# Two-block transformer kernel: last merge and gated outputs kept in PSUM, two steps moved on VectorE and TensorE

## The reference, cut to what matters

```
x   = rmsnorm(x, g_final)                      # end of the first block
h   = rmsnorm(x, g_mix)
xc, gb, gc, q, k, v, g_sw, gate_a, gate_r = split(h @ w_in)
y_a = (gb * conv3(gc * xc)) @ w_a_out          # 8 "mixing" steps
ret = retention(q, k, v)                       # 4 heads of 512 value columns
ret = (ret - mean) * rsqrt(var + eps) * g_ret
y_r = (ret * silu(g_sw)) @ w_r_out
merged = sigmoid(gate_a) * y_a + sigmoid(gate_r) * y_r
x   = x + merged @ w_o
x   = x + (silu(rmsnorm(x) @ w_ff_gate) * (rmsnorm(x) @ w_ff_up)) @ w_ff_down
out = rmsnorm(x, g_final_2)
```

## Time and profile before

| | |
|---|---|
| timed runs | 1609.0, 1609.24, 1611.55 us; median 1609.24 us |
| profiled execution, its own time | 1607.12 us |
| its span, first to last instruction | 1605.1 us |
| busy: PE, DVE, ACT, POOL | 97%, 51%, 19%, 62% of the span |
| mean granted TensorE clock | 0.989 of full speed |

### The profile page before, as it was taken

One profiled execution on the slowest core, in us unless ns is written; L12 is line 12 of the kernel. 1 busy time (PEld: TensorE's weight loads), 2 busy tenths in 40 slices (PEclk: granted clock), 3 DMA queues, 4 the chain that ended last, 5 costly groups with the idle time before them and its releaser, 6 DMA issues.

```text
span 1605.1 us, 19515 instructions
## 1 busy us (share of the span) xinstructions
PE 1560.0 (97%) x7096; PEld 1295.3 (81%) x7096; DVE 820.9 (51%) x833; ACT 303.5 (19%) x471; POOL 988.8 (62%) x784
## 2 busy tenths in 40 slices
PE   6899999999999999999999999999999999999996
PEld 5798888887887888788888888888778888888885
DVE  6775555555407566323246675576577443443014
ACT  3423111110102000212021232221222111111011
POOL 0542666667666666666647466575467666667664
PEclk9799999999999999999999999999999999999998
DMA  9791333333232333333223222232223333332321
GB/s 366 264 359 40 101 91 102 94 92 99 89 99 79 105 91 97 91 112 92 81 83 98 77 84 87 77 93 90 65 74 98 92 97 99 91 103 93 96 100 53
DMA packets 227558, 172.38 MB, mean 107 GB/s; under 512 B 5184, under 2 KB 203968, under 8 KB 226496
## 3 DMA queue, kind: packets, MB, share of 16 engines
q1 hardware_dynamic: 227520, 171.85, 34.3%
HBM read 169.73 MB, written 2.10 MB: 107 GB/s over the span
## 4 chain that ended last, share of the span: by engine, by line
PE 89%; DVE 7%; DMA 2%; issue 1%; ACT 1%; SPq 0%; POOL 0%; DVEq 0%; ACTq 0%; POOLq 0%
PE ps L529 29%; PE ps L533 29%; PE ps L532 29%; DMA mod_early<-in_w_mod 2%; DVE wide_lo L1145 1%; PE ps L573 1%; DVE res L1436 1%; DVE ps L1189 0%; DVE tmp L1268 0%; DVE tmp L1554 0%; DVE act_lo L1368 0%; DVE tmp L1364 0%; DVE act_lo L1262 0%; DVE tmp L1175 0%; DVE tmp L1256 0%
## 5 line engine op out<-in xcount | busy, mean ns | idle before, releaser
L507 POOL TENSOR_TENSOR w_lo<-raw,w_hi 128x1024 fp32r<-128x1024 f32 x248 | 623.3, 2513 | 20.7
L529 PE MATMUL ps<-act_hi,w_hi 128*128 128x512 f32 (+1 forms) x1296 | 505.9, 390 | 6.0 <-DVE act_lo L1368 2.6
L533 PE MATMUL ps<-act_lo,w_hi 128*128 128x512 f32 (+1 forms) x1296 | 501.3, 387 | 0.0
L532 PE MATMUL ps<-act_hi,w_lo 128*128 128x512 f32 (+1 forms) x1296 | 501.3, 387 | 0.0
L504 POOL TENSOR_TENSOR w_hi<-raw,zero 128x1 fp32r<-128x1 f32 x248 | 57.9, 234 | 517.4 <-PE ps L529 517.4
L529 PEld LDWEIGHTS ps<-act_hi,w_hi 128*128 128x128 f32 x1296 | 243.8, 188 | 60.3 <-issue 6.8
L532 PEld LDWEIGHTS ps<-act_hi,w_lo 128*128 128x128 f32 x1296 | 244.0, 188 | 50.4 <-issue 1.4
L533 PEld LDWEIGHTS ps<-act_lo,w_hi 128*128 128x128 f32 x1296 | 243.8, 188 | 49.4
L505 POOL TENSOR_SCALAR w_hi<-raw 128x1023 fp32r<-128x1023 f32 x248 | 267.3, 1078 | 0.0
L529 PE MATMUL ps<-wide_hi,w_hi 128*128 128x512 f32 (+2 forms) x624 | 241.8, 388 | 6.6 <-DVE wide_lo L1145 4.2
L532 PE MATMUL ps<-wide_hi,w_lo 128*128 128x512 f32 (+2 forms) x624 | 240.6, 386 | 0.0
(11 more groups left out here) (193 smaller groups left out, 1462.9 us busy)
## 6 DMA issues: line engine op xcount, KB each, us to landing
raw<-in_w_in SPq DMA_DIRECT2D x88, 512.0 KB, 4.0
raw<-in_w_ffn_up SPq DMA_DIRECT2D x44, 512.0 KB, 3.8
gates<-in_w_mod SPq DMA_DIRECT2D x20, 1024.0 KB, 10.4
raw<-in_w_ffn_down SPq DMA_DIRECT2D x22, 512.0 KB, 3.7
raw<-in_w_ff_gate SPq DMA_DIRECT2D x22, 512.0 KB, 3.9
raw<-in_w_ff_up SPq DMA_DIRECT2D x22, 512.0 KB, 3.9
raw<-in_w_ff_down SPq DMA_DIRECT2D x22, 512.0 KB, 3.7
raw<-in_w_r_out SPq DMA_DIRECT2D x16, 512.0 KB, 3.5
```

The costliest lines, as they stand in the source:

```text
L507: nc.gpsimd.tensor_tensor(w_lo[:, two, :], raw[:, slot, :], f32(w_hi[:, two, :]), SUB).then_inc(split_done, 1)
L529: ins = mm(o, w, a, start=start, stop=False)
L532: mm(o, wl, a, start=False, stop=False)
L533: return mm(o, w, al, start=False, stop=stop)
```

## The change

There are five edits.

1. `norm(1, [2, 3])` stands behind the third mixing tile and no longer behind the second.
2. TensorE's wait for `mix_free` ahead of the gates stands ahead of the third gate tile (the first bank that mixing used, 4) and no longer ahead of the first.
3. DVE's first four `gate_scale` stand ahead of the reciprocal and the eight operations that scale `res`.
4. In every head `gated` and `scaled` write, and ACT's high part and `ret_lo` read, the bank 4 + e of PSUM in place of `tmp`. So the next head's values must not be written there before `ret_ready`: that wait stands ahead of the value products, and the wait for `ret_made` ahead of the fourth projection tile is gone. In the last `ret_out` the first tile waits for the third g_sw scaling only and the second tile for the fourth.
5. In the last merge both operations of DVE write the PSUM bank that the tile came in, and the high and low parts are made from there. So a bank is free only at `merge_ready`, and tiles m = 4 to 7 of the last `ret_out` wait for `merge_ready` m - 3 in place of `mid_free`.

```diff
@@ conv_tiles
-                    if first and u == 0 and s == 1:
+                    if first and u == 0 and s == 2:
                         norm(1, [2, 3])
@@ gates, TensorE
-            pe.wait_ge(mix_free, KT - 1)
             for g in range(4):
+                if g == 2:
+                    pe.wait_ge(mix_free, KT - 1)
@@ head_projections
-                    elif u == 2 * QT - 1:
-                        pe.wait_ge(ret_made, h * VT)
                     tile(ps[:, u, :], base + u, u % 2, act_hi, act_lo).then_inc(qk_done, 1)
                 if isinstance(h, int):
                     pe.wait_ge(key_scale_made, 1)
+                else:
+                    pe.wait_ge(ret_ready, h * VT)
@@ ret_out
                 if last:
-                    pe.wait_ge(gsw_scaled, HEADS * VT)
+                    pe.wait_ge(gsw_scaled, HEADS * VT - 1)
                     pe.wait_ge(o_std, HEADS)
-                    pe.wait_ge(split_done, base + 1)
                     for m, k in [(m, k) for ks in (range(VT - 1), [VT - 1]) for m in range(2) for k in ks]:
+                        if k == 0 and m % 2 == 0:
+                            pe.wait_ge(split_done, base + m // 2 + 1)
+                        if (m, k) == (1, 0):
+                            pe.wait_ge(gsw_scaled, HEADS * VT)
                         pe.wait_ge(ret_ready, h * VT + k + 1)
@@
-                    if m >= 4:
+                    if m >= 4 and last:
+                        pe.wait_ge(merge_ready, m - 3)
+                    elif m >= 4:
                         pe.wait_ge(mid_free, (h + 1) * KT + m - 3)
@@ ScalarE
-                    hi_of(wide_hi[:, S_RET + e, :], tmp[:, e, :], ret_hi_made)
+                    hi_of(wide_hi[:, S_RET + e, :], ps[:, 4 + e, :], ret_hi_made)
...
-                hi_of(wide_hi[:, S_MERGE + m, :], gates[:, m, :], merge_hi_made)
+                hi_of(wide_hi[:, S_MERGE + m, :], ps[:, m % 4, :], merge_hi_made)
@@ VectorE (gate_scale for g in 0 to 3 moved ahead of the scaling of res)
-                    stt(out=tmp[:, e, :], in0=ps[:, 4 + e, :], scalar=col("g_ret_2", h * VT + e), in1=tmp[:, e, :],
+                    stt(out=ps[:, 4 + e, :], in0=ps[:, 4 + e, :], scalar=col("g_ret_2", h * VT + e), in1=tmp[:, e, :],
...
-                    tt(tmp[:, e, :], tmp[:, e, :], tmp[:, 6, :], MUL).then_inc(ret_made, 1)
+                    tt(ps[:, 4 + e, :], ps[:, 4 + e, :], tmp[:, 6, :], MUL).then_inc(ret_made, 1)
...
-                    tt(tmp[:, m % 2, :], ps[:, m % 4, :], gates[:, KT + m, :], MUL).then_inc(mid_free, 1)
+                    scaled_, merged = (ps[:, m % 4, :], ps[:, m % 4, :]) if last else (tmp[:, m % 2, :], gates[:, m, :])
+                    tt(scaled_, ps[:, m % 4, :], gates[:, KT + m, :], MUL).then_inc(mid_free, 1)
                     dve.wait_ge(mid_free, (h + 1) * KT + m + 1)
-                    tt(gates[:, m, :], gates[:, m, :], tmp[:, m % 2, :], ADD).then_inc(mid_added, 1)
+                    tt(merged, gates[:, m, :], scaled_, ADD).then_inc(mid_added, 1)
```

More of the change, by code:

```diff
@@ L831, in ret_out @@
                 if last:
-                    pe.wait_ge(gsw_scaled, HEADS * VT)
+                    pe.wait_ge(gsw_scaled, HEADS * VT - 1)
                     pe.wait_ge(o_std, HEADS)
-                    pe.wait_ge(split_done, base + 1)
                     for m, k in [(m, k) for ks in (range(VT - 1), [VT - 1]) for m in range(2) for k in ks]:
+                        if k == 0 and m % 2 == 0:
+                            pe.wait_ge(split_done, base + m // 2 + 1)
+                        if (m, k) == (1, 0):
+                            pe.wait_ge(gsw_scaled, HEADS * VT)
                         pe.wait_ge(ret_ready, h * VT + k + 1)
-                        ins = product(ps[:, m, :], *w_block(base % 2, 2 * k + m), ret_hi[:, k, :], ret_lo[:, k, :],
+                        ins = product(ps[:, m, :], *w_block((base + m // 2) % 2, 2 * k + m % 2), ret_hi[:, k, :], ret_lo[:, k, :],
                                       k == 0, k == VT - 1, opens=m == 0 and k == 0)
@@ L1430, in _ @@
                     dve.wait_ge(mix_ready, j + 1)
[L1433 to L1437, removed]
             def gate_scale(g, u):
@@ L1447, in _ @@
                 gate_scale(g, g)
+            dve.wait_ge(norm_std[1], 2)
+            link(nc.vector.reciprocal(tmp[:, 6, :], tmp[:, 6, :]))
+            for k in range(KT):
+                stt(out=res[:, k, :], in0=res[:, k, :], scalar=col("g_final", k), in1=tmp[:, 6, :], op0=MUL, op1=MUL
+                    ).then_inc(res_scaled, 1)
             with dve.Fori(1, 2 * KT // 4) as i:
@@ L1517, in scaled @@
                     dve.wait_ge(o_gated, h * VT + e + 1)
-                    tt(tmp[:, e, :], tmp[:, e, :], tmp[:, 6, :], MUL).then_inc(ret_made, 1)
+                    tt(ps[:, 4 + e, :], ps[:, 4 + e, :], tmp[:, 6, :], MUL).then_inc(ret_made, 1)
                 def ret_lo(e):
-                    lo_of(wide_lo[:, S_RET + e, :], tmp[:, e, :], wide_hi[:, S_RET + e, :], ret_hi_made, ret_ready, h * VT + e + 1)
+                    lo_of(wide_lo[:, S_RET + e, :], ps[:, 4 + e, :], wide_hi[:, S_RET + e, :], ret_hi_made, ret_ready, h * VT + e + 1)
                 gsw(0)
@@ L1542, in merged_lo @@
             def merged_lo(m):
-                lo_of(wide_lo[:, S_MERGE + m, :], gates[:, m, :], wide_hi[:, S_MERGE + m, :], merge_hi_made, merge_ready, m + 1)
+                lo_of(wide_lo[:, S_MERGE + m, :], ps[:, m % 4, :], wide_hi[:, S_MERGE + m, :], merge_hi_made, merge_ready, m + 1)
             def merge(h, last=False):
```

## The result

| | before | after |
|---|---|---|
| median of the timed runs (4 each, side by side) | 1610.39 us | 1594.32 us |
| lowest to highest | 1609.0 to 1613.25 | 1593.81 to 1596.26 |
| profiled execution, own time / span | 1607.12 / 1605.1 | 1593.81 / 1591.8 |

The ratio is 0.9904 [0.9889, 0.9918]: faster by 1.0%. Forecast were 1595.9 us, and 1593.8 for the profiled execution.

What follows compares the result with a forecast made beforehand. TensorE, busy 97% of the span, bounds the kernel; time comes from its stops and slow clock. Gains 1.84 + 2.30 + 9.2 = 13.3 us take the profiled 1607.12 to 1593.8 and the median to 1595.9, range 1592.5 to 1600.5.

Steps and rivals of the forecast that it cites:

- Price of an operation: DVE's operations in last head and merge: one input in PSUM makes each 0.69 us; bounds 0.645 and 2.89.
- The last head and merge: From the last head's gated outputs through w_o: shorter DVE operations and an earlier start gain 9.2 us together.
- the head's end: Last output product: last gated output ready at 1159.05 where it released TensorE at 1161.34, a gain of 2.29 us.
- the merge: Last merge into w_o: two stops and the slow clock behind them go, 6.9 us; bounds 0, 3.9, 6.9.
- my 0.7: Last output product: TensorE still stops 0.7 us after its 18 early matmuls, waiting for the last gated output.
- The other heads: Heads before the last: the wait moved to ret_ready has 15 us of cover, so worth 0.
- The slow clock: Start of w_o: clock at 0.50 behind the long stop costs 3.0 us and goes with the stop.
- my first rival: Clock falls all the same, or small new stops eat a third of the gain: 3 to 4 back, 1599.4 us; chance 0.11.
- My constant offset of 2.1: Whole kernel: timed median stands 2.1 us above the profiled execution, turning 1593.8 into 1595.9 us.
- Edit 1 was not given back: Rival in mixing: DVE's first chain meets POOL and loses over 3.1 us, giving 1597.7 us; chance 0.08.
- PSUM did free DVE of POOL: Rival denied this: low parts of 2.89 stay and the merge keeps its pace, 1605.1 to 1607 us; chance 0.06.
- operations from PSUM into PSUM were not slow: Rival in the last merge: such operations slow beside TensorE's writes, kernel slower, 1613 us at 1.4 us each; chance 0.02.
- nothing downstream took the gain: Rival behind w_o: the change does nothing, since TensorE's gain is waited for elsewhere; chance 0.03.

Runs made afterwards that it cites:

- the experiments: The changed kernel with one part taken back each time; medians 1594.51 to 1602.9 us, beside before's medians of 1608.02 (19 runs) and 1610.5 us (7 runs).
- the first experiments: Changed kernel with norm's sums, gate scalings, last head plus merge, or merge alone taken back; ratios to before 0.9941, 0.9938, 0.9969, 0.9956.
- after's second profile: The changed kernel profiled once more with nothing altered; 1595.99 us, span 1594.0 us.

## Why the prediction was right, and where it was off

**Edit 1: 1.84 forecast, 1.78 measured.** DVE's additions came 3.8 us before they were asked for (3.7 forecast); `mix_free` came at 520.38 + 1.16 = 521.5 where 521.7 was forecast, and no wait for it appeared.

**Edit 2: 0 forecast, 0.0 measured.**

**Edit 3: 2.30 forecast, 2.2 measured** without the clock. What was moved was through at 656.97 and made nothing late.

**Price of an operation: 0.69 forecast, 0.68 to 0.70 measured** for all tensor-tensor forms; the gating with a column (L1518) takes 0.76 as a median. The prediction let a long operation end one short duration behind POOL's subtraction; in its own rows it is 0.54 us (1185.05 against 1184.51), as in the changed kernel's trace.

The Trainium skill, "VectorE: DVE Perf Modes", "The TRN2 errata — SBUF-src ops pay a fixed extra latency per instruction", gives 62 cycles more for a source in PSUM. That is not borne out by these operations, which have one input in PSUM and one in SBUF: 0.682 is the median of the low part from PSUM and 0.677 the shortest with both inputs in SBUF. For work on a matmul's output the Trainium skill, same page, "Rules for kernel authors", leaves the choice to accept the PSUM source or to copy to SBUF first if many operations follow. Here the difference that a copy could win is 0.005 us an operation, and the form with both inputs in SBUF lost up to 2.2 us beside POOL.

**The last head and merge: 9.2 forecast, 9.2 in the pair of profiles (1.77 + 7.41)**, but as a sum of two kinds. Divided where the prediction divides it, at the matmul that waits for the last gated output, it is 2.34 for the head's end (2.29 forecast) and 6.84 for the merge (6.9). The stops alone, from the run with edits 4 and 5 undone and no fall of the clock, are 6.4 (6.2 by my terms). The stop that remained is 0.43 as listed; counted from start to start, as my 0.7 was, it is 0.59. `merge_ready` 1 came at 1158.59 + 0.68 = 1159.27; tile 4 asks 1.46 + 5.45 us after 1154.82, at 1161.7, so 2.5 us of slack stand against 2.3 forecast.

**The other heads: 0 forecast.** Their new waits were not undone alone; with these waits kept and the rest of edits 4 and 5 undone, the heads lasted 442.17 and 442.07 us, against 442.13 before.

**The slow clock: 3.0 forecast, 2.8 in that execution, but not a constant.** This is the step that was off. I took the stretch at 0.50 as a consequence of the stop in w_o (right) that comes whenever the stop does (wrong). At equal stops it was 6.8, 3.4, 0, 6.8 and 3.4 us long in the five profiles that have the stop of 2.4, and cost up to 2.8. And I argued against my first rival that "a stop of 2 us alone did not bring it here": at the gates the same stop of 2.04 did bring it in two of four profiles. The rival itself did not come: with the stop down to 0.43 there was no stretch from mixing to the feed-forward part in either of the changed kernel's two profiles.

**The median.** All in all, stops are 1.8 + 2.2 + 6.4 = 10.4 us of gain in the profiled executions, and there the rest is how often the clock fell. The two profiles of before have 6.8 us at 0.50 in the edited stages each, which is 2.8 and 3.2 us of time (by the stages: 73.42 - 70.60; 226.69 - 225.05 + 72.14 - 70.60). The medians differ by 16.1, 2.8 more than my sum; against the medians of before beside the experiments, taken at other times, it would be 13.7 and 16.2. My constant offset of 2.1 between an execution and the median was the other weak step: after's median stands 0.5 above its profiled execution, before's 3.3. What can be said is that among executions with one mean clock the difference is near to the stops' alone: at 0.989 before's spans, beside the first experiments, lay between 1604.1 and 1606.0, after's second profile at 1594.0, so 10.1 to 12.0 us. That the rest of the 16.1 is clock, in the edited stages and the first block, fits these numbers, but was not tested apart from them; medians of four runs leave some 2 us open as well (13.2 to 17.9 us by the interval of the ratio).

**The rivals.** Edit 1 was not given back; PSUM did free DVE of POOL; operations from PSUM into PSUM were not slow (0.695); nothing downstream took the gain, since the rest of the program lasts 375.6 us in every profile.

## What to carry to other kernels

Where an engine at its limit waits for VectorE while GpSimd subtracts in SBUF, give each late VectorE operation one input in PSUM: here its time then no longer depended on GpSimd, and leaving the result in the bank cost nothing because the next user of the bank had slack, which has to be counted tile by tile. A wait in a full queue can be moved behind work that needs nothing from it; its worth here was the stop, to 0.1 us, since the slack downstream was counted first. A stop of TensorE of some 2 us cost 1.5 to 2.8 us more in this kernel by a fall of the clock behind it, in some executions and not in others: enter it as a spread, not as a term, and compare stages over several profiles before putting a difference of that size down to an edit.

## What the runs showed that was not expected

- From the start of mixing to the feed-forward part, over fourteen profiles, stretches at the lower clock stood only behind stops of over 2 us, and behind six of ten such stops. They were 3.4 or 6.8 us long. Behind stops of 1.7 us and less there were none. What decides between the executions stays open.
- One input in PSUM is enough: `gates<-gates,ps` took 0.686 to 0.690 us eight times beside POOL's work, `gates<-gates,tmp` 0.692 to 2.174.
- ACT's high part is shorter from PSUM as well, with a median of 0.598 against 0.632 us.
